# The last recurrence pass's variance by token and its tail on GpSimd, the first pair's load at the head of the queue, and the fourth gate bank emptied earlier

## What is computed

```python
# S5: u and z are the halves of the input projection
y = s5_ssm(u, ...)                       # needs powers of exp(a*dt) per group and state
y = y * jax.nn.sigmoid(y @ w_glu + b_glu) * jax.nn.silu(z)
# end of the recurrence, per head of 64 channels and per token
mean = jnp.mean(y, axis=-1, keepdims=True)
var = jnp.mean(jnp.square(y - mean), axis=-1, keepdims=True)
y = ((y - mean) * lax.rsqrt(var + LNX_EPS)).reshape(B, S, R) * lnx_g + lnx_b
return (y + bonus) * g * jax.nn.silu(z)
# the attention of the second block, per head
s = q @ k.T + bias;  p = softmax(s);  o = p @ v;  att = o * jax.nn.silu(z_att)
```

## Time and profile before

| | before |
|---|---|
| median of 3 runs | 3063.89 us (3062.10 to 3064.82) |
| the profiled execution | 3060.55 us |
| its span | 3058.8 us |
| TensorE busy | 2973.0 us, 97% of the span |
| VectorE, ScalarE, GpSimd busy | 1378.4 (45%), 1188.8 (39%), 1638.6 us (54%) |
| mean granted TensorE clock | 0.988 of full speed |

### The profile page before, as it was taken

One profiled execution on the slowest core, in us unless ns is written; L12 is line 12 of the kernel. 1 busy time (PEld: TensorE's weight loads), 2 busy tenths in 40 slices (PEclk: granted clock), 3 DMA queues, 4 the chain that ended last, 5 costly groups with the idle time before them and its releaser, 6 DMA issues.

```text
span 3058.8 us, 53326 instructions
## 1 busy us (share of the span) xinstructions
PE 2973.0 (97%) x21096; PEld 2382.8 (78%) x21096; DVE 1378.4 (45%) x2192; ACT 1188.8 (39%) x1640; POOL 1638.6 (54%) x1355
## 2 busy tenths in 40 slices
PE   7999999999899999999999999999999999998997
PEld 5778888888788888888888878777777777775686
DVE  8888861120443132222322046456456456455612
ACT  5455652243533232323334254343343343344521
POOL 4545544454777777777774464444444444443252
PEclk9999999999999999999999999999999999998998
DMA  4666673242222222222222242232222222225522
GB/s 172 186 196 193 206 208 142 96 152 96 71 90 94 94 89 86 89 98 91 89 86 85 97 158 89 89 106 78 90 102 81 91 98 85 91 75 154 164 96 96
DMA packets 128934, 347.95 MB, mean 114 GB/s; under 512 B 61936, under 2 KB 65008, under 8 KB 98304
## 3 DMA queue, kind: packets, MB, share of 16 engines
q1 hardware_dynamic: 128784, 345.73, 34.0%
HBM read 306.07 MB, written 35.55 MB: 112 GB/s over the span
## 4 chain that ended last, share of the span: by engine, by line
PE 49%; issue 24%; POOL 20%; DVE 3%; ACT 2%; DMA 1%; POOLq 0%; SPq 0%; DVEq 0%; ACTq 0%
POOL wlo L173 17%; PE bank L196 14%; PE bank L197 14%; PE bank L198 14%; POOL g L2018 2%; PE bank L1421 1%; PE bank L1403 1%; PE bank L2123 1%; POOL wk L649 1%; PE bank L1412 1%; PE bank L2163 1%; PE bank L2197 1%; ACT whi L168 0%; POOL wk L643 0%; DVE g L2692 0%
## 5 line engine op out<-in xcount | busy, mean ns | idle before, releaser
L173 POOL TENSOR_TENSOR wlo<-wraw,whi 128x512 fp32r<-128x512 f32 (+1 forms) x896 | 1182.9, 1351 | 1161.1 <-ACT whi L168 1161.0
L196 PE MATMUL bank<-rhi,whi 128*128 128x512 f32 x3632 | 1455.1, 401 | 45.0 <-POOL wlo L173 26.5
L198 PE MATMUL bank<-rhi,wlo 128*128 128x512 f32 x3632 | 1419.3, 391 | 0.0
L197 PE MATMUL bank<-rlo,whi 128*128 128x512 f32 x3632 | 1419.2, 391 | 0.0
L196 PEld LDWEIGHTS bank<-rhi,whi 128*128 128x128 f32 x3632 | 684.3, 188 | 217.1 <-issue 43.2
L198 PEld LDWEIGHTS bank<-rhi,wlo 128*128 128x128 f32 x3632 | 684.1, 188 | 145.3
L197 PEld LDWEIGHTS bank<-rlo,whi 128*128 128x128 f32 x3632 | 685.1, 189 | 136.9 <-issue 4.3
L168 ACT ACTIVATE whi<-wraw 128x2048 fp32r<-128x2048 f32 (+2 forms) x227 | 428.3, 1887 | 449.1 <-PE bank L198 282.6
L1195 POOL TENSOR_TENSOR wraw<-wraw,vec 128x512 f32<-128x512 f32 x248 | 252.3, 1049 | 0.0
L974 DVE TENSOR_TENSOR ssum<-ssum,wk 128x512 f32<-128x512 f32 x28 | 20.6, 737 | 278.1 <-ACT wk L964 278.1
L2018 POOL TENSOR_TENSOR g<-g,wk 128x256 f32<-128x256 f32 x80 | 59.0, 759 | 108.5 <-PE bank L1791 57.2
(11 more groups left out here) (389 smaller groups left out, 3064.2 us busy)
## 6 DMA issues: line engine op xcount, KB each, us to landing
wraw<-in_wall_dram SPq DMA_DIRECT2D x223, 1024.0 KB, 4.9
g<-scr_e SPq DMA_DIRECT2D x128, 64.0 KB, 3.2
g<-in_bmat_dram SPq DMA_DIRECT2D x16, 512.0 KB, 3.9
scr_a<-ssum SPq DMA_DIRECT2D x24, 256.0 KB, 2.3
g<-in_xp_dram SPq DMA_DIRECT2D x4, 1024.0 KB, 11.0
g<-in_cmat_dram SPq DMA_DIRECT2D x16, 256.0 KB, 7.4
scr_u<-wk SPq DMA_DIRECT2D x16, 256.0 KB, 2.8
scr_y<-wk SPq DMA_DIRECT2D x16, 256.0 KB, 3.2
```

Of the source, the lines that this page charges most:

```text
L173: ins = pool.tensor_tensor(wlo[:, slot, c], wraw[:, slot, c], whi[:, slot, c].bitcast(F32), ALU.subtract)
L196: pe.matmul(out[:, :], whk, rhi[:, k, :], start=(k == first), stop=False)
L197: pe.matmul(out[:, :], whk, rlo[:, k, :], start=False, stop=False)
L198: ins = pe.matmul(out[:, :], wlk, rhi[:, k, :], start=False, stop=(k == last))
```

## The change

Four edits.

1. The last pass's variance is made by token. TensorE multiplies each 128 tokens of the squares, as the stationary operand, with two columns of the block-diagonal ones: four products of 128 x 2 that leave 128 tokens x 8 in bank 7. The root and the reciprocal are taken on 128 x 8. VectorE spreads the result over the 64 channels of a head (`tensor_copy`), TensorE transposes it back into bank 6 (`last_spread`), and VectorE scales by it and by `lnx_g` in one step (`last_scale`). The low part of the squares and its `sum_low` are gone.
2. The tail goes to GpSimd (`last_norm`): three steps, `lnx_b` having been added to `bonus` on ScalarE.
3. The first pair's load is first in SyncE's order at the handover; the mask's load moves ahead of tile 215's. `at_turn(0)` stands before the low part of tile 215.
4. `z_scale` of the fourth gate bank stands ahead of the pass of four powers, and `crq`, `ciq` are made before the powers; the end of `parameters` only raises `pw_rdy`.

```diff
-            if u == 0:
+            if u == 0 and lo > 0:
                 z_scale(d, h + 3, 3 * h + 3, 1)
...
             d.tensor_copy(et_all[:, L - 1, 0], cr[:, s_])
+            d.tensor_copy(m["crq"], cr[:, g_])
+            d.tensor_scalar(m["ciq"], ci[:, g_], sgn, -1.0, ALU.mult, ALU.mult)
             d.tensor_copy(et_all[:, L - 1, 1], ci[:, s_]).then_inc(pw_rdy, 1)
...
+                if i == 4:
+                    z_scale(d, 3, 3, 1)
...
-            d.tensor_copy(m["crq"], cr[:, g_])
-            d.tensor_scalar(m["ciq"], ci[:, g_], sgn, -1.0, ALU.mult, ALU.mult).then_inc(pw_rdy, 1)
-            d.wait_ge(pw_rdy, 2)
+            d.sem_inc(pw_rdy, 1)
...
             if not nxt:
-                d.wait_ge(rw_cs, p + 1)
-                sum_low(d, w["kk"]).then_inc(rw_sl, 1)
                 xb_add(d, 2)
...
+            else:
+                pe.wait_ge(rw_cs, p + 1)
+                for b in range(NB):
+                    ins = pe.matmul(banks[7][:, 2 * b:2 * b + 2], w["kk"][:, b * P:(b + 1) * P], w["blk"][:, 0:P:CH],
+                                    start=True, stop=True)
+                ins.then_inc(rw_vr, 1)
+
+        def last_spread(pe):
+
+            pe.wait_ge(rw_rr, 10)
+            for b in range(NB):
+                ins = pe.transpose(banks[6][:, b * P:(b + 1) * P], w["t2"][:, b * P:(b + 1) * P], ident[:, :])
+            ins.then_inc(rw_sp_, 1)
+
+        def last_recip(d):
+            d.wait_ge(rw_sd, 8)
+            d.reciprocal(w["ex"], w["ex"]).then_inc(rw_rr, 1)
+            d.wait_ge(rw_rr, 9)
+            d.tensor_copy(w["t2"].rearrange("p (g t) -> p g t", g=2 * NB), bc(w["ex"], 2, [P, 2 * NB, CH]))             .then_inc(rw_rr, 1)
+
+        def last_scale(d):
+            d.wait_ge(rw_sp_, 9)
+            d.scalar_tensor_tensor(w["lc"], w["lc"], vcol(V_LG, 7), banks[6], ALU.mult, ALU.mult).then_inc(rw_nm, 1)
+
+        def last_norm(pool):
+            pool.wait_ge(rw_nm, 11)
+            pool.wait_ge(rw_bl, 9)
+            cn = w["lc"]
+            pool.tensor_tensor(cn, cn, w["bonus"], ALU.add).then_inc(rw_pn, 1)
+            pool.wait_ge(rw_pn, E_STEPS + 1)
+            pool.tensor_tensor(cn, cn, w["g"], ALU.mult).then_inc(rw_pn, 1)
+            pool.wait_ge(rw_pn, E_STEPS + 2)
+            pool.wait_ge(rw_zs, 8)
+            pool.tensor_tensor(col(g2, 15), cn, w["zs"], ALU.mult).then_inc(rw_out, 1)
...
+            if not nxt:
+                sq.then_inc(rw_cs, 1)
+                act.activation(w["bonus"], w["bonus"], ACT.Identity, bias=vcol(V_LB, p)).then_inc(rw_bl, 1)
+                act.wait_ge(rw_vr, p + 1)
+                act.activation(w["ex"], banks[7][:, 0:2 * NB], ACT.Sqrt, bias=vec[:, V_EPSL:V_EPSL + 1], scale=1 / CH)\
+                   .then_inc(rw_sd, 1)
+                return
...
             if h == 1:
-                pe.wait_ge(rw_cn, 8)
-                pe.wait_ge(rw_sd, 8)
+                pe.wait_ge(rw_nm, 11)
...
                 if h == 0:
+                    last_spread(pe)
                     project(pe, N_B + 3, 1, range(2, NBK), wait_r=96)
...
+                if h == 0:
+                    last_recip(d)
                 at_minima(d, h)
+                if h == 0:
+                    last_scale(d)
...
                     xb_add(d, 3)
-                    rw_root(d, link, 7)
-                if h == 1:
-                    rw_norm(d, link, 7)
...
             make_lo(pool, N_B + 2, 0)
+            at_turn(pool, 0)
             make_lo(pool, N_B + 3, 1)
-            for p in range(8):
+            for p in range(1, 8):
                 at_turn(pool, p)
+                if p == 1:
+                    last_norm(pool)
...
         def at_sp(sp):
+            sp.wait_ge(rw_op, 8)
+            sp.wait_ge(a_wr, 16 + 96)
+            at_load(sp, 0)
             sp.wait_ge(a_wr, 16 + 96 * 8)
             xb_load(sp, 0)
             xb_load(sp, 1)
             w_load_next(sp, N_B + 2, 0)
+            sp.wait_ge(b_wr, 32)
+            sp.wait_ge(rw_lm, 8)
+            sp.dma_start(xt["bias"], scr_b).then_inc(p6_in, 16)
             w_load_next(sp, N_B + 3, 1)
             xb_store(sp, 0)
-            sp.wait_ge(b_wr, 32)
-            sp.dma_start(xt["bias"], scr_b).then_inc(p6_in, 16)
-            sp.wait_ge(rw_op, 8)
-            at_load(sp, 0)
             xb_load(sp, 2)
```

More of the change, by code:

```diff
@@ L1502, in program @@
         rw_out = sem("rw_out")
+        rw_rr, rw_nm, rw_sp_, rw_bl, rw_pn = rw_cn, rw_cn, rw_mu, rw_gc, e_rdy
         def shift_mix(d, link, n, src, mu, out, done, before):
@@ L1901, in rw_pe @@
             fill(7 if nxt else 4)
-            pe.wait_ge(rw_sl, 4 * p + 4)
-            head_sum(pe, banks[7]).then_inc(rw_vr, 1)
             if nxt:
+                pe.wait_ge(rw_sl, 4 * p + 4)
+                head_sum(pe, banks[7]).then_inc(rw_vr, 1)
                 fill(128)
+            else:
[27 more added lines that the diff above has]
+            pool.tensor_tensor(col(g2, 15), cn, w["zs"], ALU.mult).then_inc(rw_out, 1)
         def w2_of(k):
@@ L1994, in rw_act @@
             act.wait_ge(rw_cn, p + 1)
-            act.activation(w["kk"], w["lc"], ACT.Square)
+            sq = act.activation(w["kk"], w["lc"], ACT.Square)
+            if not nxt:
[5 more added lines that the diff above has]
+                return
             act.activation(s_hi, w["lc"], ACT.Square).then_inc(rw_cs, 1)
```

## The result

| | before | after |
|---|---|---|
| median of 5 runs each | 3062.74 us (3058.98 to 3064.82) | 3044.99 us (3044.70 to 3047.84) |
| ratio | | 0.9947, 95% interval 0.9936 to 0.9958 |
| the profiled execution, its span | 3060.55, 3058.8 us | 3044.90, 3043.1 us |
| mean granted TensorE clock | 0.988 | 0.992 |

Between the two medians the change is faster by 17.75 us. The ratio in the table, 0.9947, is not the quotient of these medians (0.9942) and stands for 16.2 us. Between the two profiled executions the span fell by 15.7 us. To see where, I cut both spans at four starts on TensorE: the second group of small state products (L546), the second product of the last pass's mean (L1727 before, L1728 after), the fifth head's scores, and the sixteenth head's scores.

What follows compares the result with a forecast made beforehand. TensorE, busy 97% of the span, was taken as the bound, its waits and low clock as the room. Handover 18.0 plus start 1.5 gave 19.5 us: 3044.4 us, own range 3042 to 3048, wider range 3040 to 3052.

Steps and rivals of the forecast that it cites:

- the 9.92 end: Handover's best end: both first head pairs take 9.92 us, the first steady pair's time, for a gain of 20.2 us.
- The load at the front: Handover: first pair's load issued from about 2740.7, landed by 2753, so the 3.87 us wait goes.
- the first wait: Handover: TensorE's 3.87 us before the first head's scores, for GpSimd's rotary addition behind a late load; claimed to go.
- the two others: Handover: waits of 2.99 and 4.93 us before the third and fourth heads' scores, traced to VectorE's reciprocal and norm.
- I leave it inside the 0.3: Handover: GpSimd's moved tail beside the first head's divide, priced within the 0.3 us added for filling the chain.
- cover until about 2781.5: Handover: the first head's divide has until about 2781.5 before anyone waits, with the tail at about 2779 to 2783.
- with a penalty of 0 to 2.2 it ends at 86.3 to 89.6: Start: end of `dve_out`, 5.3 us alone, with 0 to 2.2 us added for running beside GpSimd's low half.
- The gain of 1.5: Start: early fourth gate bank lets tile 6 start 0.5 to 2.8 us earlier; 1.5 taken as the middle.
- The stores: Rival, handover: second head's divide waits for the residual's fourth block store; gain 13.0 us, 3050.9 us; 20%.
- The chain as the bound: Rival, first heads: chain of minima, exponential, copy bounds them, so only the first wait goes; 3056.8 us; 4%.
- Slower, by a collision on each head: Rival, attention: a GpSimd instruction falls on each of 16 divides, costing 29.4 us; 3073.8 us; 2%.
- More than forecast: Rival: steady pairs at 9.92 us and the best front, 20.2 + 2.8 us; 3040.9 us; 10%.

Runs made afterwards that it cites:

- the three with another start: Changed kernel with the whole old start, with only the fourth gate bank late again, with only the coefficients late again: 3044.53, 3043.51 and 3048.12 us.
- the held low part: Changed kernel with GpSimd's low part of tile 6 held until VectorE's long product of the first output step is done: 3045.70 us, ratio 0.9952.
- the two halves: Kernel before with the new load order alone: 3052.97 us, ratio 0.9980; changed kernel with the old load order: 3055.39 us, ratio 0.9984.
- the tail on VectorE: Changed kernel with the norm's three last steps on VectorE behind the second divide, instead of on GpSimd: 3045.92 us, ratio 0.9957.
- the tail held back: Changed kernel with the old start and GpSimd's tail of the norm held until VectorE has divided the first head: 3044.77 us, ratio 0.9958.
- The start alone: Kernel before with only the changed kernel's start (early fourth gate bank and coefficients): 3057.60 us over 12 runs, ratio 0.9999.

## Why the prediction was right, and where it was not

**The handover: right, in size and in mechanism.** Forecast gain 18.0, in the profile 18.3. In the executions whose handover code is that of the changed kernel (after twice, and the three with another start, and the held low part) the stretch takes 26.3, 29.7, 25.6, 28.0, 26.8 and 28.0, so the gain is 14.9 to 19.0, on average 17.2. From the first small product (2777.52) to the fifth scores it took 23.33 us, or 22.6 without the 0.74 of the head sum that they replace, where the sum had 22.75; but it is made up differently: the pairs are near the 9.92 end (10.32 from the third to the fifth scores, with a wait of 0.36 in it), and the waits of 1.64 and 0.36 fill the rest. The load at the front, the hidden SyncE issues, the small products (0.95 instead of 0.74) all came as worked out. That the first wait is apart from the two others is shown by the two halves, 6.8 and 11.9 us. That the two others are apart from each other is shown by the tail on VectorE: the third scores do not wait there and the fourth wait 4.21 us.

**"I leave it inside the 0.3".** Too small. The tail beside the first divide cost VectorE 2.5 us (2.71 + 1.19 against 0.82 + 0.55), and the spread copy 1.5 (1.93 against 0.43); the third scores waited 1.64. The "cover until about 2781.5" was wrong, as the divide itself only began at 2783.45. With the tail held back the wait is gone, though the copy is still long (2.46), so it takes the long divide to make it. The copy sets a part of its size: with the same divide, 2.71 and 1.19, the wait was 0.93 where the copy took 0.43 (the changed kernel with the old start) and 1.64 to 1.76 where it took 1.93 to 2.48.

**The clock behind a wait.** The prediction said that each low stretch comes behind a wait, and had no new wait in its sum. One has come ahead of the sixth scores (1.25 in the profile, 0.4 to 1.8 in the others). In the nine profiles that have it, the twelve heads from the fifth to the sixteenth scores take 57.6 to 57.9 where the granted clock stayed at 1.00 (four of them), 59.3 where it was 0.96 further on (one), and 61.0 to 63.1 where it fell to 0.83 or 0.91 in the first 20 us (four). In three with no such wait they take 56.2 to 56.3; the kernel before has no such wait either and takes 58.3, with 0.96 further on. The length of the wait alone does not decide it: 1.19 us stood ahead of a low stretch, 1.25 and 1.26 did not. The medians of all versions with the full handover, 3043.5 to 3048.1, do not follow the 25.3 to 29.7 of their handovers. The twelve heads may be why, but one execution of each was profiled and the intervals of their ratios overlap, so this is not shown.

**The start: the step that failed** is "with a penalty of 0 to 2.2 it ends at 86.3 to 89.6". Two things in it were off. First, the penalty: I took it from one long product (2.44 instead of 1.35), as if a collision cost each step its own share. Measured, each short product that GpSimd was ahead of stood for about a whole instruction of it, so the price is by count, as the 7.4, 8.5 and 9.6 us above show: (1.38 + 1.38 + 1.27) - 3 x 0.28 = 3.2, and 1.1 for the long one, 4.3 us. Second, the start: 81.0 to 82.1 forecast, 83.42 in the profile. Of the 3.3 us by which the powers ended later than in the kernel before, 0.6 is `z_scale`, 0.5 a later begin of the whole program, about 1.4 the moved pair (the copy behind it took 1.28 at 61.55, beside a GpSimd instruction; inside my bound of 1.5), and 0.89 was not in my list: the fourth `z_scale` waits for the store of the third bank, because both go through the one buffer `zt`. I had counted every instruction that the moved step issues, and not what it waits for at its new place. In other executions this wait is 0.52 or absent.

The gain of 1.5 that I took is thus one side of a race. Where VectorE's three short products go first, the second group is 1.1 to 2.4 us early; where GpSimd's low part is in, it is 1.2 to 4.6 late. This is against the one profile of the kernel before, at 110.97, the earliest of the five with the old start (the latest is 112.27). The start alone measured 0.9999. The sum's own middle was 1.65 and not 1.5, which changes nothing.

**The total.** 3044.4 forecast, 3044.99 measured, and this closeness is partly luck. The gain was forecast at 19.5 us and was 17.75 between the medians and 15.7 between the profiled executions; the forecast started from a median of 3063.89, which became 3062.74 with two more runs. The profiled execution came out at 3044.90 against the 3041.05 of the sum, since the start went 6.1 us the wrong way (-1.5 forecast, +4.6 found) and 2.3 us came back elsewhere (0.3 in the handover, 0.5, 0.4 and 1.1 in the other stretches). That the median lay 3.3 us above the profiled execution held for the kernel before and not for the one after.

**The rivals.** The stores: no. The second head's divide follows VectorE's copy without an idle time, and the fourth block's store is issued at 2788.09, in time. The chain as the bound: no for the first five heads; for the third scores it is 1.64, 0.93 to 1.76 in the others. Slower, by a collision on each head: no. GpSimd did fall on some divides (1.82 and 1.83 in the fourth head), as in the kernel before. More than forecast: no, its 3040.9 lies below every run of the changed kernel, the lowest being 3043.01.

The Trainium skill's rule in "SBUF — State Buffer", section "SBUF: two separate sides", that the loser of the shared port stands until the other's whole instruction is over, is what the 1.38 us of a 0.28 us product shows. By it, applied to each of the short products and not to the long one alone, a collision at the start would have been priced at its 4.3 us.

**Still open:** the stretch from the second group to the last pass took between 2656.1 and 2661.6 us in the profiles, with no edit in it. No trace of mine says why.

## What to carry to other kernels

When a step is moved to an earlier place, list what it waits for there, its buffers too, and what its earlier end sets free: here an earlier bank freed ScalarE, which started GpSimd, which got in the way of the very step that was to gain. Price a meeting of VectorE and GpSimd by the number of VectorE instructions that can each wait for one of GpSimd's, and not by VectorE's busy time; many short steps pay most, and an order that lets the short ones go first by a microsecond is no order unless a semaphore makes it one. And look at the granted clock behind a short wait on TensorE: of nine waits of 0.4 to 1.8 us here, four stood ahead of stretches with a lower clock that took 3 to 5 us more, so a gain of one microsecond at one place need not be kept if a wait is left at another.

## What the runs showed that I had not expected

A VectorE product of 128 x 128 between SBUF operands took 0.28 us alone and 1.26 to 1.39 beside GpSimd's 128 x 512 subtractions. A copy of 128 x 512 took 0.43 us from SBUF alone, 1.93 to 2.48 from SBUF beside GpSimd's rotary addition, and 0.69 from PSUM beside the same addition. The products with one operand in PSUM (L434, L435) kept their 0.75 to 0.77 beside GpSimd's low part. One and the same program ran its start in two ways, 5.9 us apart at the second group, by whether one engine was 1.6 us ahead of the other or level with it.
